# Two transformer blocks on one core: in the projections and feed-forward parts, the last two units of every chunk are multiplied bank by bank

## The reference

```
mod = silu(c) @ w_ada + b_ada                        # six rows of 2048
h = rmsnorm(x) * (1 + sc_m) + sh_m
proj = h @ w_in                                      # 2048 x 8208: "in1"
y = concat(hgrn2(proj), gated_delta(proj)) @ w_out   # "mix1"
x = x + gt_m * rmsnorm(y)
y = square(relu(h2 @ w_ff1)) @ w_ff2                 # 2048 x 8192 x 2048: "ffn1"
x = x + gt_f * rmsnorm(y)
x = x + hybrid_mixer(rms_norm(x))                    # w_in_2 and w_out_2: "in2", "mix2"
x = x + cross_attention(rms_norm(x), mem)            # "cq", "co"
val, gate = split(h3 @ w_up)                         # 2048 x 2*5504: "ffn2"
x = x + (silu(conv3(gate)) * val) @ w_down           # 5504 x 2048
return rms_norm(x)
```

## Time and profile before

| | |
|---|---|
| median of 3 runs | 2749.26 us |
| the profiled execution's own time | 2747.99 us |
| its span | 2746.2 us |
| PE busy | 2660.4 us (97%) |
| DVE busy | 1785.0 us (65%) |
| ACT busy | 1224.8 us (45%) |
| DMA | 571.73 MB, mean 208 GB/s |

### The profile page before, as it was taken

One profiled execution on the slowest core, in us unless ns is written; L12 is line 12 of the kernel. 1 busy time (PEld: TensorE's weight loads), 2 busy tenths in 40 slices (PEclk: granted clock), 3 DMA queues, 4 the chain that ended last, 5 costly groups with the idle time before them and its releaser, 6 DMA issues.

```text
span 2746.2 us, 32675 instructions
## 1 busy us (share of the span) xinstructions
PE 2660.4 (97%) x12618; PEld 2160.7 (79%) x12618; DVE 1785.0 (65%) x2178; ACT 1224.8 (45%) x1572; POOL 69.3 (3%) x92
## 2 busy tenths in 40 slices
PE   5899999899999999999999999999999999999998
PEld 3478887787888888888887777788888888888896
DVE  7887677995785555555577355667665565656576
ACT  2155645343444444444444455544654434343443
POOL 1000000001000000000000100000000000000000
PEclk9999999999999999999999999999999999999999
DMA  9988887355595555555574544444455555555553
GB/s 375 370 291 272 313 304 252 138 192 210 197 359 185 197 184 183 184 197 183 183 292 169 185 152 153 139 154 161 162 199 188 190 187 186 183 188 179 199 173 119
DMA packets 166944, 571.73 MB, mean 208 GB/s; under 512 B 9993, under 2 KB 30648, under 8 KB 162609
## 3 DMA queue, kind: packets, MB, share of 16 engines
q1 hardware_dynamic: 161936, 544.25, 57.9%
q0 software_dynamic: 4720, 25.57, 2.6%
q10 hardware_dynamic: 176, 0.40, 0.1%
HBM read 562.58 MB, written 7.60 MB: 208 GB/s over the span
## 4 chain that ended last, share of the span: by engine, by line
PE 61%; issue 28%; DVE 7%; DMA 2%; ACT 2%; POOL 0%; SPq 0%; DVEq 0%; POOLq 0%; ACTq 0%
PE banks L475 17%; PE banks L477 17%; PE banks L476 17%; DMA raw_weights<-in_w_ada 2%; PE banks L592 1%; DVE mod_in L1019 1%; PE banks L932 1%; ACT weights_high L424 1%; DVE proj L1231 1%; DVE weights_low L437 1%; PE banks L893 1%; PE banks L1952 1%; DVE proj L1215 0%; PE banks L1153 0%; DMA first_weights<-in_w_in 0%
## 5 line engine op out<-in xcount | busy, mean ns | idle before, releaser
L437 DVE TENSOR_TENSOR weights_low<-raw_weights,weights_high 128x1024 fp32r<-128x1024 f32 (+2 forms) x814 | 966.9, 1197 | 729.3 <-ACT weights_high L424 721.8
L424 ACT ACTIVATE weights_high<-raw_weights 128x1024 fp32r<-128x1024 f32 (+2 forms) x814 | 838.8, 1037 | 929.4 <-PE banks L477 888.4
L475 PE MATMUL banks<-weights_high,lhs_high 128*128 128x512 f32 (+1 forms) x2264 | 897.7, 396 | 7.8 <-DVE lhs_low L605 2.2
L477 PE MATMUL banks<-weights_high,lhs_low 128*128 128x512 f32 (+1 forms) x2264 | 880.4, 389 | 0.0
L476 PE MATMUL banks<-weights_low,lhs_high 128*128 128x512 f32 (+1 forms) x2264 | 878.9, 388 | 0.0
L475 PEld LDWEIGHTS banks<-weights_high,lhs_high 128*128 128x128 f32 x2264 | 425.7, 188 | 100.6 <-issue 8.6
L477 PEld LDWEIGHTS banks<-weights_high,lhs_low 128*128 128x128 f32 x2264 | 425.3, 188 | 88.5
L476 PEld LDWEIGHTS banks<-weights_low,lhs_high 128*128 128x128 f32 x2264 | 426.1, 188 | 82.1 <-issue 1.2
L475 PE MATMUL banks<-weights_high,hid_high 128*128 128x512 f32 x768 | 300.6, 391 | 3.0 <-DVE y_rows L574 1.7
L476 PE MATMUL banks<-weights_low,hid_high 128*128 128x512 f32 x768 | 299.0, 389 | 0.0
L477 PE MATMUL banks<-weights_high,hid_low 128*128 128x512 f32 x768 | 299.0, 389 | 0.0
(11 more groups left out here) (429 smaller groups left out, 2069.2 us busy)
## 6 DMA issues: line engine op xcount, KB each, us to landing
raw_weights<-in_w_ff SPq DMA_DIRECT2D x128, 1024.0 KB, 5.0
raw_weights<-in_w_ada SPq DMA_DIRECT2D x96, 1024.0 KB, 6.9
raw_weights<-in_w_in SPq DMA_DIRECT2D x96, 1024.0 KB, 5.4
raw_weights<-in_w_up SPq DMA_DIRECT2D x80, 1024.0 KB, 5.0
raw_weights<-in_w_down SPq DMA_DIRECT2D x42, 1024.0 KB, 5.1
raw_weights<-in_w_out SPq DMA_DIRECT2D x32, 1024.0 KB, 5.2
first_weights<-in_w_in SPq DMA_DIRECT2D x16, 768.0 KB, 12.0
raw_weights<-in_w_up SPq DMA_DIRECT2D x16, 384.0 KB, 3.8
```

Source lines behind the costliest of these rows:

```text
L424: act.activation(WHI[:, u % SPN, 0:c.width], raw_unit(c, n, k), ACT.Copy).then_inc(S("high_made"), 1)
L437: dve.tensor_tensor(WLO[:, u % SPN, 0:c.width], raw_unit(c, n, k), WHI[:, u % SPN, 0:c.width].bitcast(F32), ALU.subtract).then_inc(S("low_ ...
L475: nc.tensor.matmul(o, x, hi, start=(k == 0), stop=False)
L477: mm = nc.tensor.matmul(o, y, hi, start=False, stop=(k == c.kn - 1))
```

## The change

One list gets longer: `staggered` is set for all chunks of in1 (`segs` holds these alone at that point), mix1, ffn1 and ffn2, the chunks in loops among them.

```
-        for c in stages["cq"][0][1]:
+        for c in [c for _, chunks in segs for c in chunks] + [c for name in ("mix1", "ffn1", "ffn2") for _, chunks in stages[name] for c in chunks] + \
+                stages["cq"][0][1]:
             c.staggered = True
```

## The result

The changed kernel takes 2865.61 us, median of 4 runs (2862.89 to 2868.32), against 2749.42 (2748.29 to 2749.9) before: ratio 1.0423, 95% interval 1.0405 to 1.0441. It is 116 us slower. The forecast was 2844 with a range from 2824 to 2868, so the time lies inside, near the upper end; it lies above the 2836 to 2856 of the forecast's own account (stalls with 3 to 14 falls of the clock) and in the 2857 to 2880 of the rival with a fall at most places. The profiled execution took 2868.32 us with a span of 2866.4, 120.2 more than before.

The account below looks back on a forecast made before the run. The prediction took PE, busy 97% of the span, as the bound. Stalls of 55.1 + 16.9 + 4.2 + 6.6 = 82.8 us plus 12 for clock falls made 95 us, so 2844 us against the median, range 2824 to 2868.

Parts of the forecast that it names:

- the forecast's own account: Where chunks meet: stalls of 82.8 us plus 3 to 14 clock falls, 2836 to 2856 us; chance 0.50.
- the rival with a fall at most places: Stalls plus clock falls at most or all places, 27 falls giving 2878 us; band 2857 to 2880, chance 0.12.
- The chain and the delay: At chunk ends, copy of unit 2 starts 2.04 us later; PE restarts at 2.71 (DVE) or 1.43 us (ACT).
- the 15 undivided ones: DVE's places without four transposes in the gap, PE idle 2.3 us; about half, 7, have clock falls: 12 us.
- The moved wait: PE waits for the last unit's low part 2.72 us earlier; put at nothing, up to 5 us in gate chunks.
- the sign of being wrong that the prediction names: Within chunks: waits appearing at line 476 for weights_low would show the prediction wrong; no size given.
- The banks after the first don't add: At PE's restart, banks come free 0.59 or 0.62 us apart and PE needs them 0.68 apart: no cost.
- No falls: Rival: stalls as forecast, but the clock falls 0 to 2 times; 2832 us, chance 0.28.
- a fall at each place: Rival's extreme, from the Trainium skill's rule: a clock fall at each of the 53 places, 2922 us.
- Only waits above 2 us had falls: Argument against falls at most or all places, from the earlier trace: 2.05 us idle had one, 1.80 none.
- Half absorbed: Rival: PE has unseen slack at these places or unit 2's copy is released earlier; 2790 us, chance 0.07.
- Not slower: Rival: bank 0's take-out follows its earlier completion at once, the 25 waits go, 12.6 us; 2737 us, chance 0.03.

Follow-up runs that it names:

- the one with matmuls in ten waits: Changed kernel plus 8 extra matmuls into an unused bank ahead of unit 0 in ten second down chunks; 2854.08 us, ratio 1.0383.
- the one with the added results only: Kernel before, with the flag new only for the 27 chunks whose results DVE adds or multiplies into rows; 2829.99 us, ratio 1.0293.
- the two with the old order: Kernel before with take-out after unit 1, 2739.63 us; the same with PE waiting for the last unit's low part one unit earlier, 2747.72 us.
- the kernel by halves: Changed kernel with the last two units done half by half, freeing unit kn-2's slot 6 matmuls before the end, not 3; 2807.97 us, ratio 1.0213.

## Why the prediction was right, step by step

The range holds the time, and the mechanism of the stalls is the one that the runs show. The account of the clock is not: it was 15 us too low, and that is most of the 22 us between 2844 and the measured time.

- **The chain and the delay.** Where DVE adds, the restart is at 2.71 us in the loops, as worked out, and at 2.87 at most places outside them, where it had been 0.83; the delay is 2.03 to 2.04 at 25 of the 27 places, and 1.80 and 1.75 at two late in ffn2. Where ACT copies, the restart is at 1.34 to 1.49 us in in1 and ffn1 and at 1.43 to 1.58 in ffn2 for the 1.43 expected. By kind the places give 54.5 us (55.1 expected), 16.9 (16.9), 4.6 (4.2) and, in1, 6.4 (6.6), together 82.4 for the 82.8 forecast. In in1 that is luck in part: the three places taken at 0.5 each measured 0.95, 0.47 and 0.
- **The clock.** Here the forecast was too low: "about half of the 15 undivided ones, 7: 12 us". The runs showed 17 falls, 27 us. 12 of the 15 undivided waits had one, and 5 of the 12 with four transposes in the gap, which I took to be safe. So the forecast's own case, 3 to 14 falls, didn't come true: with 17 falls at 27 places the rival "at most or all of the places" did, to which I gave 0.12, and in its band the time lies. The doubt that I drew from the small matmuls beside the wait of 2.05 us in the earlier trace rows went the wrong way. The price of one, 1.7 from the earlier trace rows, measured 1.6. Why a wait has a fall in one execution and the same wait none in another stays open: over the changed kernel, the one with matmuls in ten waits and the one with the added results only, 25 of 35 undivided waits without such matmuls had one, and 14 of 36 with four transposes.
- **The moved wait.** "I put it at nothing", with up to 5 us in gate chunks held in the range: it was 4.1 us of idle time (5 from start to start), in four gate chunks of ffn2 and, the longest with 1.4, one chunk of in1. That is the sign of being wrong that the prediction names, waits for `weights_low` within chunks. They stand at the start of the last two units. In the gate chunks ACT's last copies stand behind a step of its own that waits for DVE's conv and gate work; in in1 a table load on ACT and small steps beside it stand ahead of the last copy. A gate chunk near its end, on ACT and then on PE, and the table load in in1:

```profile
2348.66 0.63 ACT L2904 ACTIVATE modulation<-modulation 128x512 f32<-128x512 f32 x1 [5.41 <-DVE modulation L2931]
```

```profile
2351.55 0.50 PE L476 MATMUL banks<-weights_high,lhs_high 128*128 128x512 f32 x1 [0.77 <-DVE weights_low L438]
```

```profile
309.56 1.28 ACT L1433 ACT_TABLE_LOAD   x1
```

- **What the sum left out.** Some 6 us. "The banks after the first don't add" was wrong by a little: PE's first steps behind ACT's copies are paced by them (up to 0.16 us a place, 2 in all). And from ffn1's end to ffn2 the clock is low for longer, 2.6 us. The profiled executions of all eight experiments have 1.3 to 3.0 us there, the two with the old order 1.6 and 1.5, so part of it at least is no matter of the order; nothing here tells what it is.
- **The rivals.** "No falls" is out by the trace, a fall at each place by the count: 18 of the 53, 17 in ffn1 and ffn2 and one in the mixer behind in1's last chunk. "Only waits above 2 us had falls" didn't hold as it stood: five falls lie behind waits of 1.9 to 2.0 us and, in the kernel by halves, one behind 1.8. The Trainium skill's rule on oscillation from cycling through banks (TensorE: Matmul & The Clock Gate, A second HAM failure mode: psum-queue depth-cycling) holds for the waits of 2.3 us and not for those of 0.3 to 0.7 us before nor for 1.0 us after. "Half absorbed" had no slack to live on. "Not slower" was right in one thing: the old waits could go, and a take-out ahead of unit 2's copy does it, but that needs no new order. It is 2739.63 us against the 2737 that I worked out for it, which is near by luck: the 12.6 us counted nine waits twice and left out the places with transposes and what a wait costs beyond its idle time.

## What to carry to other kernels

Before an order is changed so that results are complete earlier, look at what stands ahead of their consumer in its own queue, and which buffer that one waits for: here the earlier banks were worth nothing, because the slot of the old chunk's last unit but one came free 2.04 us later and everything behind it in ACT's and DVE's order moved along. The cheaper cure for a wait at a boundary was to move the take-out one step ahead in the consumer's order, with matmuls untouched. And between dense matmuls a wait of PE above 2 us cost more than its length here: 1.6 us more for about seven in ten of them.

## What the hardware showed that I had not expected

Behind 12 of 15 waits that left PE idle for 2.3 to 2.5 us between dense matmuls, the granted clock went from 2.4 to 1.2 GHz for 8 matmuls or so, 1.6 us lost each. With four transposes in the gap, which leave 1.6 to 2.0 us, it was 5 of 12. In the kernel by halves, with waits of 0.9 to 1.8 us, it was 1 of 27; behind ACT's copies in the changed kernel, with 1.25 us at the longest, it was none of 24, in1's last chunk aside, where PE waited 2.7 us and the clock fell; and with eight matmuls of no use put into the wait it was none of 10. Work without a purpose in a wait that can't be avoided thus gained 11.5 us over ten places.

Idle time is not the only thing that did it. Between ffn1 and ffn2 the clock of the changed kernel fell behind six matmuls on 33 rows, with PE busy all the time:

```profile
1596.67 2.46 PE L2318 MATMUL banks<-modulation 33*128 33x384 f32 x6
```

```profile
1599.60:1603.60 4.00, 4.00 (x12) 2.85 (x10) 1.23 (x1) 1.00 (x2) 0.54 (x1) 0.57 0.55 166
```

The eight matmuls that kept the clock up were of full size, 128 x 512. Whether small ones would have done it, no run shows.
